# Attention woven into dense matmuls: a fourth tile of scores, and three slots instead of two between scores and transpose

## What is computed

```python
def chunk_band_attention(q, k, v, rel_bias):      # first block, 8 heads
    ...
    scores = jnp.einsum('bcqhd,bckhd->bhcqk', q, kb).astype(jnp.float32) * scale
    ...
    scores = scores + bias[None, :, None]
    scores = jnp.where(valid[None, None, :, None, :], scores, -1e30)
    probs = jax.nn.softmax(scores, axis=-1).astype(v.dtype)
    out = jnp.einsum('bhcqk,bckhd->bcqhd', probs, vb)

def forgetting_attention(q, k, v, f_logit, b_f):  # second block, 16 heads
    ...
    for i in range(S // Q_BLOCK):
        ...
        s = s + cum[:, :, lo:hi, None] - cum[:, :, None, :hi]
        s = jnp.where(kpos[None, :] <= qpos[:, None], s, -1e30)
        prob = jax.nn.softmax(s, axis=-1).astype(v.dtype)
        outs.append(jnp.einsum('bhqk,bhkd->bhqd', prob, v[:, :, :hi]))
```

## Time and profile before

| | before |
|---|---|
| median of 3 runs | 1647.4 us (1646.85 to 1647.98) |
| the profiled execution | 1648.76 us; span of its instructions 1646.8 us |
| TensorE busy | 1612.9 us, 98% of the span |
| VectorE, ScalarE, GpSimd busy | 963.0, 672.3, 171.4 us |
| attention calls, us from the start | 1: about 230 to 316; 2a: 768 to 843; 2b: 964 to 1041 |

### The profile page before, as it was taken

How to read it: one execution, slowest core, us unless ns; L and a number is a source line. 1 busy time by engine, 2 the same in 40 slices (tenths; PEclk the granted TensorE clock), 3 DMA queues, 4 the chain that set the end, 5 groups by cost and what they waited for, 6 DMA issues and landing times.

```text
span 1646.8 us, 19120 instructions
## 1 busy us (share of the span) xinstructions
PE 1612.9 (98%) x7624; PEld 1332.8 (81%) x7624; DVE 963.0 (58%) x1452; ACT 672.3 (41%) x1011; POOL 171.4 (10%) x242
## 2 busy tenths in 40 slices
PE   7999999999999999999999999999999999999998
PEld 6878778788888888888788877888888888888787
DVE  6745688674343434746844568544567727735757
ACT  5534475543222313513672146442334414414544
POOL 0001136200000000003710146000000000000000
PEclk9999999999999999999999999999999999999999
DMA  5224231122222222332122221322232222222321
GB/s 187 77 77 148 84 128 52 52 103 102 92 88 102 103 102 83 122 129 77 52 78 102 77 77 52 128 102 83 96 116 102 94 86 103 102 102 85 120 103 52
DMA packets 27992, 157.30 MB, mean 96 GB/s; under 512 B 3776, under 2 KB 6272, under 8 KB 10752
## 3 DMA queue, kind: packets, MB, share of 16 engines
q1 hardware_dynamic: 23184, 145.52, 24.9%
q10 hardware_dynamic: 4720, 10.56, 1.8%
HBM read 151.84 MB, written 4.23 MB: 95 GB/s over the span
## 4 chain that ended last, share of the span: by engine, by line
PE 87%; DVE 7%; issue 2%; ACT 2%; POOL 2%; DMA 0%; POOLq 0%; SPq 0%; DVEq 0%; ACTq 0%
PE bank L586 24%; PE bank L588 24%; PE bank L587 24%; PE bank L594 2%; PE bank L596 2%; PE bank L595 2%; PE bank L787 1%; PE bank L772 1%; PE bank L883 1%; DVE w_lo L1613 1%; DVE w_lo L1620 1%; POOL k_blk L511 1%; PE bank L758 1%; PE bank L1059 0%; PE bank L759 0%
## 5 line engine op out<-in xcount | busy, mean ns | idle before, releaser
L586 PE MATMUL bank<-a_hi,w_hi 128*128 128x512 f32 x1184 | 465.7, 393 | 9.3 <-DVE w_lo L1814 8.7
L588 PE MATMUL bank<-a_hi,w_lo 128*128 128x512 f32 x1184 | 462.1, 390 | 0.0
L587 PE MATMUL bank<-a_lo,w_hi 128*128 128x512 f32 x1184 | 461.9, 390 | 0.0
L1104 ACT ACTIVATE w_hi<-w_raw 128x2048 fp32r<-128x2048 f32 x120 | 228.9, 1908 | 280.4 <-DMA w_raw<-in_strips 277.1
L1613 DVE TENSOR_TENSOR w_lo<-w_raw,w_hi 128x2048 fp32r<-128x2048 f32 x118 | 270.2, 2290 | 16.5 <-ACT w_hi L1104 16.4
L586 PEld LDWEIGHTS bank<-a_hi,w_hi 128*128 128x128 f32 x1184 | 223.0, 188 | 54.7 <-DVE w_lo L1814 8.7
L588 PEld LDWEIGHTS bank<-a_hi,w_lo 128*128 128x128 f32 x1184 | 222.9, 188 | 46.9
L587 PEld LDWEIGHTS bank<-a_lo,w_hi 128*128 128x128 f32 x1184 | 223.1, 188 | 44.9 <-issue 0.2
L586 PE MATMUL bank<-b_hi,w_hi 128*128 128x512 f32 x560 | 218.2, 390 | 1.1 <-DVE w_lo L1613 0.6
L587 PE MATMUL bank<-b_lo,w_hi 128*128 128x512 f32 x560 | 217.9, 389 | 0.0
L588 PE MATMUL bank<-b_hi,w_lo 128*128 128x512 f32 x560 | 217.9, 389 | 0.0
(11 more groups left out here) (328 smaller groups left out, 2094.3 us busy)
## 6 DMA issues: line engine op xcount, KB each, us to landing
w_raw<-in_strips SPq DMA_DIRECT2D x132, 1024.0 KB, 4.8
seg_in<-cum_kept ACTq DMA_DIRECT2D x16, 256.0 KB, 3.5
x<-in_x_t SPq DMA_DIRECT2D x4, 512.0 KB, 7.2
head_bias<-in_rel ACTq DMA_DIRECT2D x1, 2048.0 KB, 10.9
x_kept<-x ACTq DMA_DIRECT2D x1, 2048.0 KB, 6.9
x<-x_kept SPq DMA_DIRECT2D x1, 2048.0 KB, 10.4
out<-out_t SPq DMA_DIRECT2D x12, 128.0 KB, 1.7
w_raw<-in_strips SPq DMA_DIRECT2D x4, 256.0 KB, 6.2
```

What stands on the lines that cost most here:

```text
L586: mm(ps[:, :], w_hi[slot][:, k, cols], hi[:, k, :], start=(k == 0), stop=False)
L587: mm(ps[:, :], w_hi[slot][:, k, cols], lo[:, k, :], start=False, stop=False)
L588: return mm(ps[:, :], w_lo[slot][:, k, cols], hi[:, k, :], start=False, stop=(k == kt - 1))
L1104: run(w_hi[j], w_raw[j], ACT.Copy).then_inc(hi_split, 1)
```

## The change

It gives each tile of `score` a buffer of its own, four in all (the fourth lies apart from the other three), and puts one more slot between `scores(n)` and everything from `turn(n)` on: slot n turns tile n - 3, round n keeps tile n - 4, values, copying and adding of rows and the splits of finished heads come one slot later, and there are 37 slots. The tables of pieces are dealt out anew.

```diff
-SLOTS = TILES + 4
-
-SLOT_PIECES = [5, 3, 2] + [44 * (n + 1) // 29 - 44 * n // 29 for n in range(29)] + [2, 2, 3, 3]
+SLOTS = TILES + 5
+
+SLOT_PIECES = [5, 3, 2, 2] + [42 * (n + 1) // 28 - 42 * n // 28 for n in range(28)] + [2, 2, 2, 2, 2]
...
-LEAD_PIECES = [0, 0, 3, 2] + [49 * (n + 1) // 28 - 49 * n // 28 for n in range(28)] + [2, 2, 3, 3]
+LEAD_PIECES = [0, 0, 3, 2, 2] + [47 * (n + 1) // 27 - 47 * n // 27 for n in range(27)] + [2, 2, 2, 2, 2]
...
-            return {"score": sb(f"score_{call}", [P, 3, T], at=at),
+
+            return {"score": [sb(f"score_{call}_{j}", [P, T], at=work + 8192 if j == 3 else at + j * T) for j in range(4)],
...
-                        last = tr(bank[4 + n % 2][:, j * P:(j + 1) * P], score[:, n % 3, j * P:(j + 1) * P], ident)
+                        last = tr(bank[4 + n % 2][:, j * P:(j + 1) * P], score[n % 4][:, j * P:(j + 1) * P], ident)
...
-                    if 2 <= n < TILES + 2:
-                        turn(n - 2)
-                    if n >= 5 and n % 4 == 1 and n < TILES + 4:
-                        values((n - 5) // TT, 0)
-                    if n >= 7 and n % 4 == 3:
-                        values((n - 7) // TT, 1)
+                    if 3 <= n < TILES + 3:
+                        turn(n - 3)
+                    if n >= 6 and n % 4 == 2:
+                        values((n - 6) // TT, 0)
+                    if n >= 8 and n % 4 == 0:
+                        values((n - 8) // TT, 1)
...
-                    if 3 <= n < TILES + 3:
-                        keep(n - 3)
+                    if 4 <= n < TILES + 4:
+                        keep(n - 4)
                     if n < TILES and (n or lead is None):
                         exps(n)
-                    if n >= 8 and n % TT == 0:
-                        copy_rows((n - 8) // TT)
-                    if not causal and (n in (15, 23, 31) or n == SLOTS + 1):
-                        split_first((n - 8) // 8)
+                    if n >= 9 and n % TT == 1:
+                        copy_rows((n - 9) // TT)
+                    if not causal and (n in (16, 24, 32) or n == SLOTS + 1):
+                        split_first((n - 9) // 8)
...
-                    if n >= 3:
-
-                        dve.wait_ge(turned, t0 + n - 2)
+                    if n >= 4:
+
+                        dve.wait_ge(turned, t0 + n - 3)
...
                     if 1 <= n < TILES + 1:
                         invert(n - 1)
-                    if 3 <= n < TILES + 3:
-                        keep(n - 3)
-                    if 8 <= n <= SLOTS and n % TT == 0:
-                        add_rows((n - 8) // TT)
-                    if not causal and (n in (15, 23, 31) or n == SLOTS + 1):
-                        split_first((n - 8) // 8)
+                    if 4 <= n < TILES + 4:
+                        keep(n - 4)
+                    if 9 <= n <= SLOTS and n % TT == 1:
+                        add_rows((n - 9) // TT)
+                    if not causal and (n in (16, 24, 32) or n == SLOTS + 1):
+                        split_first((n - 9) // 8)
                     if n < TILES - TT and n % TT in (1, 2):
                         stage(n // TT + 1, n % TT - 1)
```

More of the change, by code:

```diff
@@ L517, in normalize @@
                     pool.wait_ge(inverted, TILE0[call] + n + 1)
-                    pool.tensor_scalar(score[:, n % 3, 0:w], score[:, n % 3, 0:w], row_inv[:, n:n + 1], 1.0,
+                    pool.tensor_scalar(score[n % 4][:, 0:w], score[n % 4][:, 0:w], row_inv[:, n:n + 1], 1.0,
                                        ALU.mult, ALU.mult).then_inc(normed, 1)
@@ L1152, in exps @@
                     act.wait_ge(maxed, t0 + n + 1)
-                    run(score[:, n % 3, 0:w], score[:, n % 3, 0:w], ACT.Exp, bias=row_max[:, n:n + 1], scale=-1.0,
+                    run(score[n % 4][:, 0:w], score[n % 4][:, 0:w], ACT.Exp, bias=row_max[:, n:n + 1], scale=-1.0,
                         accum_out=row_sum[:, n:n + 1]).then_inc(exped, 1)
@@ L1745, in most @@
                     src = bank[2 + n % 2][:, 0:w]
-                    if n >= 3:
-                        dve.wait_ge(turned, t0 + n - 2)
+                    if n >= 4:
+                        dve.wait_ge(turned, t0 + n - 3)
                     added = future[:, T - w:T] if causal else head_bias[:, head * T + T - w:head * T + T]
-                    v.tensor_tensor_reduce(score[:, n % 3, 0:w], src, added, -1.0, 3.0e38,
+                    v.tensor_tensor_reduce(score[n % 4][:, 0:w], src, added, -1.0, 3.0e38,
                                            ALU.add, ALU.min, row_max[:, n:n + 1]).then_inc(maxed, 1)
```

## The result

| | before | after |
|---|---|---|
| median | 1647.26 us (8 runs) | 1652.44 us (1651.57 to 1653.35, 8 runs) |
| ratio to before, 95% interval | | 1.0032 [1.0022, 1.0041] |
| span of the profiled execution | 1646.8 us | 1651.5 us |
| call 1, first scores to last values | 86.3 us | 87.3 us |
| call 2a | 74.6 us | 77.7 us |

The forecast was no change, 1648.0, in a range of 1642.5 to 1652.0. The time lies outside, on the slow side. The stretches between and behind the three calls are the same to 0.1 us; the one ahead of call 1, which the change doesn't touch, varies by 1.9 us from one profile to the next (228.6 to 230.5 over all the kernels here), so kernels are compared by their medians and by the length of the three calls.

A forecast was written before the change was run, and what follows sets the result against it. TensorE, busy 98% of the span, was taken as the bound. Call 1 at 0, 2a at +0.25 and 2b at +0.4 us summed to +0.6 us on the 1647.4 us median: 1648.0 us, no change, range 1642.5 to 1652.

The forecast's parts named there:

- the rival that the turns would still wait for GpSimd: TensorE's turns: the change doesn't do what it says and they still wait for GpSimd's row; chance 1%.
- the 0.15 us at 806.11: Call 2a before the change: a wait for VectorE's low part standing 0.15 us behind the turn's wait for GpSimd.
- my sum: Round-by-round count of VectorE's lateness: call 1 0, call 2a +0.25, call 2b +0.4, together +0.6 us.
- The 0.7 us that I gave the fourth scores of call 1: Call 1, slot 3: its scores wait 0.7 us for `most`, with a wait on `row_max` as the sign.
- the normalised tile has a slot more: Turns on TensorE: some 2.0 us more room, so waits on GpSimd go, -13.2 us if nothing else binds.
- 3.02 us: VectorE's round 1 of a head after the change, forecast at 3.02 us, for 1.65 before.
- the margin of 0.25 us: Plain heads: VectorE's third low part is ready at 6.66, the turn needing it stands at 6.97; margin 0.25 us.
- C: Rival: plain heads' low part is 0.4 us late, TensorE waits in 7 heads of each call; +6 us, 1653.5; 18%.
- A: Rival: the rotation costs VectorE nothing, and the low part alone bounds the gain; -5.3 us, 1642; 20%.
- Bursts: Four rounds running with parts of a strip's split, four times a call; some 15 us in all on each side.
- A sign that couldn't tell: TensorE's idle time in the three stretches of the calls stays as before within 1.5 us each.
- The rule of the Trainium skill: VectorE's split parts in bursts, contending with GpSimd: 0.7 us a burst more than the 0.9 taken, or 0.9 less.

The follow-up runs named there:

- the second profile: The changed kernel itself, unaltered, measured and profiled again beside the other kernels on one chip: 1652.39 us, ratio 1.0029 to the kernel before.

## Why the prediction was wrong

**The waits that go.** Right: all 16 waits on the normalised score are gone, and the rival that the turns would still wait for GpSimd fell.

**What stands in their place.** Half right. I read from the 0.15 us at 806.11 that the low part would be waited for, and at the turns of two blocks in slots 4k; it is, in 10 places, eight of them such turns. But my sum made the turns lose 16 us after the change (3.35, 6.25 and some 6.4), about as before, and they lose 7.8. TensorE reaches those turns later, because it has already waited at the scores just ahead: with the copy early the scores lose less and the turns 12.3. The 0.7 us that I gave the fourth scores of call 1 behind `row_max` came out as 0.8.

**The step that failed** is the sentence that the normalised tile has a slot more, so that the waits on GpSimd go. It looked at one thing that the late reciprocal holds up and not at what is queued behind it. In calls 2a and 2b GpSimd's list has the next head's last q copy behind the normalising of tile 4k + 1, and TensorE needs that copy at slot 4k + 4, with two slots as with three. In the kernel before, the turn of tile 4k + 1 and eight value products (0.97 us) stood ahead of those scores and covered the copy; the change puts a turn of one block there, which covers 0.03 us. The part on the change named the order on VectorE and TensorE and never went through GpSimd's, though the wait at 971.12 shows it. The sum had nothing for new waits of a head's first scores. They lose 11.3 us where they lost 0.8, of which the copy is 8.6 (in the second profile 10.4), and late splits and copies of k in call 1 2.7.

**The size of round 4k + 1.** I took 3.02 us. Eight of the nine plain rounds take 3.1 to 3.3: there the wait for the rows' copy is 0.74 to 0.90 us, mostly 0.89, for my 0.79, and in some the split of q is longer by up to 0.17. That alone uses up the margin of 0.25 us, or nearly. In the head shown it is 4.1: 0.67 us of waiting for ScalarE's `pt_hi` come on top, and 0.36 us by which the split of q is longer while GpSimd copies k (1.07 against the 0.71 of the earlier trace rows), while the wait for the rows' copy is 0.68. So the round was nearly right, and a margin of a quarter of a microsecond was no basis for a term of 0.

**The rivals.** C came nearest: plain heads wait, and the time is +5.2 us for the +6 it gave. The agreement of the two numbers is in part luck. It priced 0.4 us at the low part in every head; that is right for call 1, where the turns of slots 8, 12 and so on to 28 all wait for it. In 2a and 2b the waits are mostly at the first scores, behind the same round, and only a third of what these lose is in plain heads. I gave it 18%. What spoke for it, a margin of 0.25 us at the end of a sum of three rounds with two waits in them, deserved more. A fell for the change itself; once the rows are added elsewhere, which takes most of the rotation's cost from VectorE, the kernel measures -4.1 us, for the -5.3 by which A was bounded.

**Bursts.** I put nearly all costs after the change into them. By the second profile that is right for less than half of what the first scores of 2a and 2b lose, 4.4 of 10.4 us. Spreading them moved the changed kernel by 0.9 us (0.4 against the kernel before of each series), within the intervals, but it put quarters into other long rounds too.

**A sign that couldn't tell.** I had named TensorE's idle time in the three stretches, the same as before within 1.5 us each. It was, while the calls grew by 1.0, 3.1 and 2.4 us. Idle is 6.4, 3.1 and 4.9 us now, for 5.6, 2.4 and 4.3 in the earlier trace rows:

```profile
226.00:321.00 95.00, 88.65 (x498) 72.80 (x497) 77.66 (x199) 56.66 (x131) 42.35 (x64) 1.00 0.16 56
757.00:847.00 90.00, 86.94 (x474) 72.46 (x473) 64.86 (x171) 52.88 (x126) 42.73 (x65) 0.98 0.15 51
955.00:1048.00 93.00, 88.10 (x478) 73.11 (x477) 68.31 (x182) 51.24 (x120) 44.60 (x65) 0.98 0.17 57
```

The records hide 0.27 us of each wait of first scores, and at the lower clock TensorE is busy for longer with the same work. The length of a call, or times from start to start, would have told.

**Two engines at SBUF.** The split of q, with two inputs in SBUF, took 1.07 us at 996.26 beside GpSimd's `k_blk` copy. In the run with the rows added late it took 0.72 at 987.36, and the normalising of 128 columns that GpSimd did beside it took 0.68 us, for 0.37 at 995.04 in the changed kernel beside no such instruction. The rule of the Trainium skill ("SBUF — State Buffer", "Who interferes with whom") is that a VectorE instruction with two SBUF inputs contends with a GpSimd instruction that reads SBUF. Both traces agree with it, in another place than I weighed it for, and with either engine as the one that waits.

## What to carry to other kernels

When a pipeline gets a stage of distance more, everything behind it is rotated against what is not: go through the list of each engine round by round, the one of the helper too, and ask for each result that becomes late what else is queued behind it. A wait in the middle of an in-order list can cost more than the work beside it (5.6 us against 0.4 in calls 2a and 2b); put an addition that needs another engine's copy a few rounds after the copy, where it finds it done. The longer distance alone lost 5 us (1652.4), the adding in the lightest round alone won 2 (1645.4), and both together won 4 (1643.3), against 1647.3 to 1647.6 for neither. And look at more than one head: the one that shows the chain best here was the worst of nine.

## What the runs showed of the hardware that was not expected

In the first profile of the changed kernel the granted clock was at its lower level, 1.2 of 2.4 GHz, in two places behind waits. Columns: stretch, its length, busy us of PE, PEld, DVE, ACT and POOL with counts, PEclk, DMA share, GB/s:

```profile
806.00:810.00 4.00, 2.64 (x12) 1.45 (x10) 3.94 (x11) 1.72 (x4) 1.73 (x3) 1.00 0.11 47
810.00:812.00 2.00, 1.76 (x9) 1.79 (x10) 1.87 (x7) 1.21 (x6) 1.01 (x2) 0.58 0.00 0
812.00:814.00 2.00, 2.00 (x9) 1.76 (x9) 0.83 (x4) 0.52 (x2) 1.73 (x4) 0.56 0.03 8
814.00:816.00 2.00, 2.00 (x13) 1.64 (x12) 1.24 (x2) 1.17 (x3) 1.53 (x3) 1.00 0.00 0
```

Three waits in a row, which cost 0.22, 1.09 and 0.88 us over the stall-free pitch, end at 807.22, 808.34 and 810.24; then the matmuls of 512 columns follow each other in 0.42 us, not 0.23:

```profile
812.78 0.63 PE L595 MATMUL bank<-w_hi,a_hi 128*128 128x512 f32 x1
813.20 0.63 PE L596 MATMUL bank<-w_lo,a_hi 128*128 128x512 f32 x1
813.63 0.45 PE L597 MATMUL bank<-w_hi,a_lo 128*128 128x512 f32 x1
```

The same happens near 1012. The profile of the changed kernel taken again has the same waits there (0.28, 1.09 and 0.88 us in call 2a) and a clock of 1.00, and its calls 2a and 2b are 1.2 and 0.6 us shorter. So these waits don't always bring the lower clock, and that they brought it in the first profile is not shown, only that it came right behind them. Nor is the clock the cause of the result. The medians of the two series are the same, 1652.4, and in the first the two runs with a mean clock of 0.995 took 1653.2 and 1653.4 us, those with 0.998, the clock of the kernel before, 1651.6 and 1651.9, which is still over 4 us slower than before. The lower clock is a cost on top, some 0.9 us for each place as an estimate from the two profiles.
